# A routed layer's x rows and its results: one transfer over 128 partitions in place of four over 32

## Chip, cores and metric

The program runs on one core of a Trainium2 chip. The metric is the time of one execution on the device, in microseconds (us). The core has five engines with instruction streams of their own: TensorE (PE, with PEld for its weight loads), VectorE (DVE), ScalarE (ACT), GpSimd (POOL) and SyncE (SP). The data between memory and the core's SBUF is moved by 16 DMA engines, which the profile shows as a share of busy time (mean over the 16) and as GB/s.

## What is computed

One layer of a hybrid trunk for 1,024 prompt tokens and 32 sample tokens of 1,024 numbers each. A token mixer (gated linear attention beside differential attention) gives `x1 = x + gate1 * mix`; then a channel mixer takes, for each token, 128 of 16,384 single-neuron experts and adds their weighted sum. Only the second part's frame matters here:

```python
x = x + gt1[:, None, :] * mix
h2 = modulate(x, norm2_gain, sh2, sc2)
ff = peer_ffn(h2.reshape(B * L, D_MODEL), w_pq, sub_keys1, sub_keys2, peer_u, peer_v)
x = x + gt2[:, None, :] * ff.reshape(B, L, D_MODEL)
...
act = jax.nn.gelu(jnp.einsum('td,thkd->thk', xt, peer_u[idx]), approximate=False)
return jnp.einsum('thk,thkd->td', g * act, peer_v[idx])
```

`peer_u` and `peer_v` lie side by side in memory, so that one gathered row of 8 KB has both vectors of an expert.

## The kernel before

The tokens are worked on in nine tiles of up to 128 rows, in five groups (`GROUPS`). The dense part of each group (projections, attention, gates) streams its weights in 1 MB blocks through `NW = 3` buffers `w`, which SyncE refills as TensorE lets go of them (L1742). The routed part is cut into 33 units of 32 tokens (`NU = 33`, `T = 32`). The 128 experts of each of the 32 tokens are spread over 128 partitions: partition `a * 32 + t` has quarter `a` of token `t`'s list (`COPIES = 4`). A unit is 32 gathers (`COLS`), each of 128 rows of 8 KB into one of `RING = 9` slots (`rt_ring`, L1716), issued by GpSimd. Two gathers make a batch, so a unit has `NB = 16` batches.

For each batch VectorE multiplies the gathered `u` halves with the tokens and sums (L1662), ScalarE applies the gelu (L1217), VectorE writes the diagonal matrices (L1673) and TensorE accumulates the `v` halves (L890). With that a pair of slots is free, and GpSimd's wait on `added` ends. The dense work of the next group is laid between the batches by a plan (`sequence`), in a fixed order on each engine, so a late batch also makes the dense work behind it late, and the other way round.

What the change touches is at the edges of a unit. `unit(u)` on SyncE loads what the unit needs: the normed tokens (`rt_h`, L1909), indices and shares (`rt_few_idx`, L1912; `rt_few_prob`, L1915), each in four pieces, and the rows of `x1` (`rt_x`, L1919). The accumulated result of a unit is folded so that partition `a * 32 + t` has columns `a * 256` to `a * 256 + 255` of token `t` (`QC = 256`), and `rt_x` and `rt_y` have the same shape, 128 partitions by 256 numbers. `finish(u)` on VectorE multiplies with the gate and adds `rt_x` (L1687, L1689), in batch 4 of the next unit. `store(u)` on SyncE waits for it and writes `rt_y` to the output (L1926), in batch 6. Before it loads `rt_x` for unit u, SyncE waits until unit u - 2 is finished, since there are two buffers of each. SyncE works off all of this and the weight loads in one queue, in program order.

Of the kernel before, what the change touches and what calls it, by code (L numbers as in the profile page):

```python
# [42 lines left out]
T, COPIES = DEC, P // DEC  # L43
# [3 lines left out]
QC = D // COPIES  # L47
UNITS = [(t * P + j * T, t, j) for t in range(NT) for j in range(COPIES)] + [(SEQ, NT, 0)]
NU = len(UNITS)
# [300 lines left out]
def trunk(nc, d):  # L350
# [15 lines left out]
    with ExitStack() as ctx:  # L366
        def sb(name, shape, dt=F32):
            return ctx.enter_context(nc.sbuf_tensor(name, shape, dt))

        def sem(name, software_dma=False):  # L370
            if software_dma:
                return nc.alloc_semaphore(name)
            used.append(ctx.enter_context(nc.semaphore(name)))
            return used[-1]
# [25 lines left out]
        def area(start, size, *dims):  # L400
            ap = arena[:, start:start + size]
            if len(dims) == 1:
                return ap.rearrange("p (a c) -> p a c", a=dims[0])
            if len(dims) == 2:
                return ap.rearrange("p (a b c) -> p a b c", a=dims[0], b=dims[1])
            return ap
# [18 lines left out]
        x1, h2T = area(0, 2 * D, 2), area(2048, KC * NCOL, KC)  # L425
# [26 lines left out]
        xr = [sb(f"rt_x1{u}", [P, QC]) for u in range(2)]  # L452
        y = [sb(f"rt_y{u}", [P, QC]) for u in range(2)]
# [45 lines left out]
        idx_in, prob_in, tokens_in, rows_in, y_out = ([sem(f"rt_{n}{u}") for u in range(2)]  # L499
                                                      for n in ("idx_in", "prob_in", "tokens_in", "rows_in", "y_out"))  # L500
# [748 lines left out]
        def _(dve):  # L1249
# [415 lines left out]
            def weigh(b):  # L1665
                u, q = b // NB, b % NB
                if q == 0:
                    dve.wait_ge(prob_in[u % 2], 16 * COPIES * (u // 2 + 1))
                dve.wait_ge(gelued, b + 1)
                if b >= 2:  # L1670
                    dve.wait_ge(added, b - 1)
                for i in range(B):
                    dg = nc.vector.tensor_scalar(diag[b % 2][:, i, :], stack, act_dot[:, b % 2, i:i + 1],  # L1673
                                                 few_prob[u % 2][:, q * B + i:q * B + i + 1], ALU.mult, ALU.mult)
                dg.then_inc(weighted, 1)
                if q == 4 and u > 0:
                    finish(u - 1)

            def finish(u):
                i = u % 2  # L1680
                dve.wait_ge(folded, u + 1)
                if u == 0:
                    dve.wait_ge(gate2_in, 16 * 2 * COPIES)
                if u >= 2:
                    dve.wait_ge(y_out[i], 16 * COPIES * (u // 2))
                dve.wait_ge(rows_in[i], 16 * COPIES * (u // 2 + 1))
                nc.vector.tensor_tensor(y[i][:], acc[i][:, 0:QC], gate2[:, 0 if u < NU - 1 else 1, :], ALU.mult).then_inc(gated2, 1)  # L1687
                dve.wait_ge(gated2, u + 1)
                nc.vector.tensor_tensor(y[i][:], y[i][:], xr[i][:], ALU.add).then_inc(y_ready, 1)  # L1689
# [4 lines left out]
            for kind, *args in order("vector"):  # L1694
# [6 lines left out]
                elif kind in stages:  # L1701
                    stages[kind](*args)
            finish(NU - 1)

        @block.gpsimd
# [14 lines left out]
        def _(sp):  # L1720
# [23 lines left out]
            def stored(g):  # L1744

                for i in range(VBUF):
                    sp.wait_ge(v_out[i], 32 * values_stored(g, i))
                for i in range(KBUF):
                    sp.wait_ge(kt_out[i], 16 * (g + 1))
# [150 lines left out]
            def unit(u):  # L1900
                row, t, j = UNITS[u]
                g = [t in tiles for tiles in GROUPS].index(True)
                i = u % 2
                if u >= 2:
                    sp.wait_ge(weighted, (u - 1) * NB)
                for k in range(2):
                    sp.wait_ge(h2_out[k], 16 * sum(s % 2 == k for s in range(GROUPS[g][-1] + 1)))
                sp.wait_ge(x1_out, 16 * (GROUPS[g][-1] + 1))
                sp.dma_start(h2[i][0:T, :], d["h2"][row:row + T]).then_inc(tokens_in[i], 16)  # L1909
                sp.wait_ge(idx_ready, t + 1)  # L1910
                for a in range(COPIES):
                    sp.dma_start(few_idx[i][a * T:(a + 1) * T, :], idx[t % 2][j * T:(j + 1) * T, a * COLS:(a + 1) * COLS]).then_inc(idx_in[i], 16)  # L1912
                sp.wait_ge(prob_ready, t + 1)
                for a in range(COPIES):
                    sp.dma_start(few_prob[i][a * T:(a + 1) * T, :], share[t % 2][j * T:(j + 1) * T, a * COLS:(a + 1) * COLS]).then_inc(prob_in[i], 16)  # L1915
                if u >= 2:
                    sp.wait_ge(y_ready, u - 1)
                for a in range(COPIES):
                    sp.dma_start(xr[i][a * T:(a + 1) * T, :], d["x1"][row:row + T, a * QC:(a + 1) * QC]).then_inc(rows_in[i], 16)  # L1919

            def store(u):
                row = UNITS[u][0]
                sp.wait_ge(y_ready, u + 1)
                dst = d["y_prompt"][0, row:row + T] if u < NU - 1 else d["y_sample"][0]
                for a in range(COPIES):
                    sp.dma_start(dst[:, a * QC:(a + 1) * QC], y[u % 2][a * T:(a + 1) * T, :]).then_inc(y_out[u % 2], 16)  # L1926

            def weigh(b):
                if b % NB == 6 and b // NB > 0:
                    store(b // NB - 1)  # L1930

            stages = {"modrow": modrow, "norm": norm, "dv": dv, "state": store_state, "state2": store_state2, "merge": merge, "mix": mix,
                      "shift": shift, "keys": keys, "gates": gates, "unit": unit, "weigh": weigh}
            for item in order("sync"):
                kind, *args = item
# [4 lines left out]
                for name in finished(item):  # L1940
                    if WPOS[name] + NW < len(WEIGHTS):
                        load_weights(WPOS[name] + NW)
            store(NU - 1)
            sp.wait_ge(y_out[0], 16 * COPIES * ((NU + 1) // 2))
            sp.wait_ge(y_out[1], 16 * COPIES * (NU // 2))
            stored(NG - 1)
            for i in range(3):
                sp.wait_ge(kr_out[i], 16 * max(rows_stored(r) for r in range(NG * 8) if r % 3 == i))
# [78 lines left out]
```

## Time and profile before

| what | value |
|---|---|
| median of 3 runs | 4189.8 us (4176.69 to 4191.25) |
| the profiled execution's own time | 4194.65 us |
| its span | 4192.6 us |
| busy, share of the span | PE 74%, PEld 47%, DVE 65%, ACT 35%, POOL 30% |
| moved | 1499.18 MB, mean 358 GB/s |
| transfers that load `rt_x` | 132 of 32.0 KB |
| transfers that store `rt_y` | 132 of 32.0 KB (128 prompt, 4 sample) |

The busy shares are means over stages with different limits. PE is the engine busiest over the whole span, yet in the last tenth of it PE is busy three tenths of the time. A stretch is bounded by what ends the waits there, so the prediction goes by stretches. A DMA share of 1.00 or a little above means that all 16 engines had a packet in hand all the time (packets overlap a little in the records).

### The profile page before, as it was taken

How to read it: one execution, taken by the hardware profiler on the slowest of the kernel's cores; microseconds unless marked ns; L12 is line 12 of the kernel's file. 1: busy time of each engine (PE TensorE's matmuls, PEld its weight loads, DVE VectorE, ACT ScalarE, POOL GpSimd, SP SyncE). 2: the span in 40 equal slices, each digit the busy share in tenths (PEclk: the TensorE clock that was granted, in tenths of full speed). 3: DMA queues.
4: the chain of work that ended last, by engine and by line, in shares of the span. 5: the costliest groups of instructions: out<-in, count | busy, mean ns of one | idle time of the engine just before them, and what ended most of it. 6: DMA issues, size and time to landing. Idle time of an engine off the chain costs nothing. (4 is left out here: it accounts for less than half of the span.)

```text
span 4192.6 us, 48832 instructions
## 1 busy us (share of the span) xinstructions
PE 3095.6 (74%) x15864; PEld 1988.9 (47%) x15864; DVE 2707.9 (65%) x7617; ACT 1464.8 (35%) x3016; POOL 1241.5 (30%) x1068
## 2 busy tenths in 40 slices
PE   6787798888787769787787789787777686633333
PEld 5677575666555437455554357454343363400000
DVE  2326347337777874578779854697787745887755
ACT  3433356312355660123445630243446611110110
POOL 0000111112233332333333332333333323355453
PEclk8798888899887979888888889898787798855555
DMA  7485767778889999999898999999999999999998
GB/s 268 170 317 180 305 231 272 264 300 336 347 341 369 388 377 394 407 413 402 341 377 351 383 409 392 416 399 397 397 376 382 413 405 414 389 415 415 399 417 335
DMA packets 269364, 1499.18 MB, mean 358 GB/s; under 512 B 44968, under 2 KB 81672, under 8 KB 97464
## 3 DMA queue, kind: packets, MB, share of 16 engines
q0 software_dynamic: 152064, 1107.36, 65.8%
q1 hardware_dynamic: 117048, 388.70, 24.5%
q8 instruction: 128, 2.10, 0.2%
q14 instruction: 124, 1.02, 0.1%
HBM read 1463.49 MB, written 31.36 MB: 357 GB/s over the span
## 5 line engine op out<-in xcount | busy, mean ns | idle before, releaser
L1716 POOL DMA_INDIRECT rt_ring<-in_peer_uv,rt_few_idx x1056 | 1238.1, 1172 | 2922.4 <-PE rt_acc L890 2293.4
L1662 DVE SCALAR_TENSOR_TENSOR rt_ring<-rt_ring,rt_h 128x1024 f32<-128x1024 f32 x1056 | 1266.6, 1220 | 495.3 <-DMA rt_ring<-in_peer_uv,rt_few_idx 488.3
L890 PE MATMUL rt_acc<-rt_ring,rt_diag 128*32 128x512 f32 x4224 | 745.9, 780 | 598.3 <-DVE rt_diag L1673 591.3
L640 PE MATMUL pair<-dense,w 128*128 128x256 f32 (+2 forms) x3056 | 596.6, 354 | 37.3 <-DMA w<-in_weights 35.6
L640 PEld LDWEIGHTS pair<-dense,w 128*128 128x128 f32 x3056 | 516.9, 198 | 149.6 <-issue 62.4
L1217 ACT ACTIVATE rt_act_dot<-rt_dot 128x2 f32<-128x2 f32 x528 | 107.2, 203 | 1299.9 <-DVE rt_ring L1662 1278.0
L629 PE MATMUL pair<-w,dense 128*128 128x256 f32 (+1 forms) x2320 | 548.6, 394 | 5.8 <-DVE dense L1318 2.8
L890 PEld LDWEIGHTS rt_acc<-rt_ring,rt_diag 128*32 128x32 f32 x4224 | 98.9, 121 | 923.9 <-DVE rt_diag L1673 782.3
L629 PEld LDWEIGHTS pair<-w,dense 128*128 128x128 f32 (+1 forms) x2320 | 428.8, 188 | 153.9 <-issue 70.5
L1673 DVE TENSOR_SCALAR rt_diag<-cst,rt_act_dot,rt_few_prob 128x32 f32<-128x32 f32 x1056 | 266.4, 297 | 70.8 <-ACT rt_act_dot L1217 37.8
L640 PE MATMUL bank<-dense,w 128*128 128x256 f32 (+2 forms) x1424 | 281.8, 355 | 19.5 <-DMA w<-in_weights 19.0
L640 PEld LDWEIGHTS bank<-dense,w 128*128 128x128 f32 x1424 | 240.2, 196 | 77.7 <-issue 32.2
L629 PE MATMUL bank<-w,dense 128*128 128x256 f32 (+1 forms) x1136 | 264.6, 389 | 8.5 <-DMA w<-in_weights 4.9
L629 PEld LDWEIGHTS bank<-w,dense 128*128 128x128 f32 (+1 forms) x1136 | 207.3, 185 | 74.2 <-issue 30.8
L1217 ACT ACT_TABLE_LOAD x170 | 218.1, 1283 | 3.0
L799 PE MATMUL pair<-w,dense 64*128 64x512 f32 (+5 forms) x416 | 150.5, 660 | 68.2 <-ACT dense L1156 63.0
L734 PE MATMUL pair<-dense 128*128 128x16 f32 (+1 forms) x528 | 96.3, 329 | 87.1 <-DVE dense L1450 87.1
L734 PEld LDWEIGHTS pair<-dense 128*128 128x128 f32 (+1 forms) x528 | 99.0, 283 | 104.3 <-issue 101.2
L819 PE MATMUL bank<-w,dense 128*128 128x128 f32 (+2 forms) x640 | 123.0, 345 | 29.2 <-DVE dense L1477 28.9
L819 PEld LDWEIGHTS bank<-w,dense 128*128 128x128 f32 (+2 forms) x640 | 102.4, 235 | 63.1 <-issue 61.3
L799 PEld LDWEIGHTS pair<-w,dense 64*128 64x128 f32 (+1 forms) x416 | 65.0, 216 | 133.5 <-issue 124.3
L1156 ACT ACTIVATE dense<-pair,negmax 128x128 f32<-128x128 f32 (+8 forms) x144 | 104.8, 731 | 55.3 <-PE bank L775 40.3
(241 smaller groups left out, 3254.2 us busy)
## 6 DMA issues: line engine op xcount, KB each, us to landing
w<-in_weights SPq DMA_DIRECT2D x284, 1024.0 KB
rt_ring<-in_peer_uv,rt_few_idx POOLq DMA_INDIRECT x1056
dense<-scratch_mod SPq DMA_DIRECT2D x18, 512.0 KB, 11.3
dense<-in_x_prompt SPq DMA_DIRECT2D x16, 512.0 KB
rt_h<-scratch_h SPq DMA_DIRECT2D x33, 128.0 KB
rt_x<-scratch_x SPq DMA_DIRECT2D x132, 32.0 KB
out_k_prompt<-dense SPq DMA_DIRECT2D x32, 128.0 KB
out_v_prompt<-dense SPq DMA_DIRECT2D x32, 128.0 KB, 6.3
```

The lines of the kernel that those rows point to most:

```text
L629: mm = nc.tensor.matmul(bank[b][0:n, 0:CH], src[:, k, c0:c0 + n], wt[:, k * CH:(k + 1) * CH], start=(k == 0), stop=(k == KC - 1))
L640: mm = nc.tensor.matmul(bank[b][:, 0:n], wt[:, k * CH + j * P:k * CH + (j + 1) * P], src[:, k, 0:n], start=(k == 0), stop=(k == KC - 1))
L734: mm = nc.tensor.matmul(bank[b][0:n, i * GBLK:(i + 1) * GBLK], k_blk[:, i, 0:n], e_blk[:, x % 2, i * GBLK:(i + 1) * GBLK], start=True, sto ...
L799: mm = nc.tensor.matmul(pair[m][0:n, o + c:o + c + w], qd[rows, h, c0:c0 + n], keys_of[rows, c:c + w], start=True, stop=True)
L819: mm = nc.tensor.matmul(bank[5][0:n, 0:VD], mixT[0:w, G % 2, (kt - first) * P:(kt - first) * P + n], v[0:w, kt, :], start=(kt == 0), stop= ...
L890: mm = nc.tensor.matmul(acc[u % 2][a * T:(a + 1) * T, :], diag[b % 2][:, i, :], slot[:, D + c * BANK:D + (c + 1) * BANK], start=(q == 0), ...
L1156: nc.scalar.activation(prob[0:n, x % 2, m, 0:nk], pair[m][0:n, o:o + nk], ACT.Exp, bias=negmax[0:n, x % 2, m:m + 1], accum_out=total[0:n, ...
L1217: nc.scalar.activation(act_dot[:, b % 2, :], dot[:, b % 2, :], ACT.Gelu).then_inc(gelued, 1)
L1662: dt = nc.vector.scalar_tensor_tensor(up, up, 1.0, h2[u % 2][:], ALU.mult, ALU.mult, accum_out=dot[:, b % 2, i:i + 1])
L1673: dg = nc.vector.tensor_scalar(diag[b % 2][:, i, :], stack, act_dot[:, b % 2, i:i + 1], few_prob[u % 2][:, q * B + i:q * B + i + 1], ALU.m ...
L1716: nc.gpsimd.indirect_dma_start(ring[n % RING][:], None, d["peer_uv"], bass.IndirectOffsetOnAxis(ap=few_idx[u % 2][:, c:c + 1], axis=0)).th ...
```

## The change

Where four transfers of 32 partitions by 256 numbers each loaded `rt_x`, one now loads all 128 partitions; the memory side is described as a view with the quarter outermost, then the token, then 256 columns. The four stores of `rt_y` are made one in the same way. The counts that are waited for on the two semaphores become a quarter. Bytes and the rows of 1 KB that they are made of stay the same.

```diff
                 if u >= 2:
-                    dve.wait_ge(y_out[i], 16 * COPIES * (u // 2))
-                dve.wait_ge(rows_in[i], 16 * COPIES * (u // 2 + 1))
+                    dve.wait_ge(y_out[i], 16 * (u // 2))
+                dve.wait_ge(rows_in[i], 16 * (u // 2 + 1))
...
                 if u >= 2:
                     sp.wait_ge(y_ready, u - 1)
-                for a in range(COPIES):
-                    sp.dma_start(xr[i][a * T:(a + 1) * T, :], d["x1"][row:row + T, a * QC:(a + 1) * QC]).then_inc(rows_in[i], 16)
+                sp.dma_start(xr[i][:], d["x1"][row:row + T].rearrange("t (a c) -> a t c", a=COPIES)).then_inc(rows_in[i], 16)
...
                 dst = d["y_prompt"][0, row:row + T] if u < NU - 1 else d["y_sample"][0]
-                for a in range(COPIES):
-                    sp.dma_start(dst[:, a * QC:(a + 1) * QC], y[u % 2][a * T:(a + 1) * T, :]).then_inc(y_out[u % 2], 16)
+                sp.dma_start(dst.rearrange("t (a c) -> a t c", a=COPIES), y[u % 2][:]).then_inc(y_out[u % 2], 16)
...
-            sp.wait_ge(y_out[0], 16 * COPIES * ((NU + 1) // 2))
-            sp.wait_ge(y_out[1], 16 * COPIES * (NU // 2))
+            sp.wait_ge(y_out[0], 16 * ((NU + 1) // 2))
+            sp.wait_ge(y_out[1], 16 * (NU // 2))
```

On SyncE, in the middle of the program, this is the end of one unit's loads and the store of the unit before, with what stands between (`w<-in_weights` is a weight block, `dense<-scratch_mod` a row of gains); the shape is that of the side written:

```order
 L1912 DMA rt_few_idx<-rt_idx 32x32 x4
 L1915 DMA rt_few_prob<-rt_prob 32x32 x4
-L1919 DMA rt_x<-scratch_x 32x256 x4
+L1918 DMA rt_x<-scratch_x 128x1x256
 L1742 DMA w<-in_weights 128x2048
 L1873 DMA dense<-scratch_mod 128x1024
-L1926 DMA out_y_prompt<-rt_y 32x256 x4
+L1924 DMA out_y_prompt<-rt_y 4x32x256
 L1880 DMA scratch_h<-dense 128x1024
 L1881 DMA scratch_x<-dense 128x1024
```

Nothing changes place: a weight block still stands behind the load of `rt_x`, and two other stores behind that of `rt_y`, now with one transfer ahead of them where there were four.

At the end of the program SyncE has, before, the last units' loads and stores:

```order
L1926 DMA out_y_prompt<-rt_y 32x256 x4
L1909 DMA rt_h<-scratch_h 32x1024
L1912 DMA rt_few_idx<-rt_idx 32x32 x4
L1915 DMA rt_few_prob<-rt_prob 32x32 x4
L1919 DMA rt_x<-scratch_x 32x256 x4
L1926 DMA out_y_prompt<-rt_y 32x256 x8
L1926 DMA out_y_sample<-rt_y 32x256 x4
```

And with the change:

```order
L1924 DMA out_y_prompt<-rt_y 4x32x256
L1909 DMA rt_h<-scratch_h 32x1024
L1912 DMA rt_few_idx<-rt_idx 32x32 x4
L1915 DMA rt_few_prob<-rt_prob 32x32 x4
L1918 DMA rt_x<-scratch_x 128x1x256
L1924 DMA out_y_prompt<-rt_y 4x32x256 x2
L1924 DMA out_y_sample<-rt_y 4x32x256
```

Again only the counts differ: eight stores of the last two prompt units are two, and the last four are one. The streams of PE, DVE, ACT and POOL are the same before and after.

## Rows read from the trace of the kernel before

**Rows 1.** The page, the DMA engines' busy tenths in 40 slices.

```profile
DMA  7485767778889999999898999999999999999998
```

**Rows 2.** The page, the chain of waits that ended last, shares by engine.

```profile
DMA 19%; PE 14%; DVE 7%; issue 3%; ACT 1%; POOL 1%; SPq 0%; DVEq 0%; ACTq 0%; POOLq 0%
```

**Rows 3.** Windows, instructions on rt_y alone (two a unit); last columns: DMA share, GB/s.

```profile
core 0: us, DVE busy (x), PEclk, DMA share, GB/s
0.00:1500.00 1500.00, 5.05 (x12) 0.86 0.78 294
1500.00:2000.00 500.00, 4.22 (x10) 0.89 0.99 398
2000.00:2400.00 400.00, 2.53 (x6) 0.84 0.92 365
2400.00:2900.00 500.00, 4.22 (x10) 0.90 1.01 404
2900.00:3200.00 300.00, 2.52 (x6) 0.78 0.96 379
3200.00:3700.00 500.00, 3.37 (x8) 0.80 1.01 407
3700.00:4150.00 450.00, 5.06 (x12) 0.50 1.01 412
...
```

**Rows 4.** The chain of waits in the last stretch: start us, us, what.

```profile
4067.76 10.94 DMA rt_ring<-in_peer_uv,rt_few_idx
4082.67 10.94 DMA rt_ring<-in_peer_uv,rt_few_idx
4097.58 11.92 DMA rt_ring<-in_peer_uv,rt_few_idx
```

**Rows 5.** Timeline of SyncE's queue: start us, us, transfers issued.

```profile
3795.82 1.71 SPq L1919 DMA_DIRECT2D rt_x<-scratch_x  x4
3797.57 1.81 SPq L1926 DMA_DIRECT2D out_y_prompt<-rt_y  x4
...
4045.33 1.71 SPq L1919 DMA_DIRECT2D rt_x<-scratch_x  x4
...
4181.91 1.71 SPq L1926 DMA_DIRECT2D out_y_sample<-rt_y  x4
```

**Rows 6.** The page, DMA packets and queues.

```profile
DMA packets 269364, 1499.18 MB, mean 358 GB/s; under 512 B 44968, under 2 KB 81672, under 8 KB 97464
...
q0 software_dynamic: 152064, 1107.36, 65.8%
q1 hardware_dynamic: 117048, 388.70, 24.5%
```

**Rows 7.** DMA issues of SyncE, 48 rows in all, 1171 transfers.

```profile
w<-in_weights SPq DMA_DIRECT2D x284, 1024.0 KB
...
rt_few_idx<-rt_idx SPq DMA_DIRECT2D x132, 4.0 KB
rt_few_prob<-rt_prob SPq DMA_DIRECT2D x132, 4.0 KB
...
scratch_mod<-rt_ring SPq DMA_DIRECT2D x16, 2.0 KB
...
rt_ring<-in_norm_gain SPq DMA_DIRECT2D x8, 2.0 KB
...
w<-scratch_kT SPq DMA_DIRECT2D x8, 16.0 KB
...
rt_ring<-in_b_mod SPq DMA_DIRECT2D x4, 12.0 KB
...
c_raw<-in_c_sample SPq DMA_DIRECT2D x1, 4.0 KB, 1.9
```

**Rows 8.** The chain of waits, two loads of a weight block: start us, us, what.

```profile
2852.95 22.90 DMA w<-in_weights
...
3407.78 23.58 DMA w<-in_weights
```

**Rows 9.** Who waited for whom: us in total, times, longest.

```profile
POOL rt_ring L1716 <- PE rt_acc L890: 2293.4, 485, 25.4
...
DVE rt_ring L1662 <- DMA rt_ring<-in_peer_uv,rt_few_idx: 488.3, 341, 9.4
...
PE pair L640 <- DMA w<-in_weights: 35.6, 5, 17.5
```

## The prediction

> **What bounds the kernel now.** I read the page's row of the DMA engines first [rows 1]: from slice 9 of 40 on it stands at 8 or 9 tenths almost throughout. The chain of waits [rows 2] has DMA as its largest share, 19% against 14% for PE, and most of the DMA part is gathers. Both are averages, so I cut the span into stretches and counted the units in each by the two VectorE instructions on `rt_y` that end a unit [rows 3]. Four stretches are full: 1500 to 2000, 2400 to 2900, 3200 to 3700 and 3700 to 4150, with a DMA share of 0.99 to 1.01. They hold (10 + 10 + 8 + 12) / 2 = 20 of the 33 units. The other 13 lie in stretches at 0.78, 0.92 and 0.96, or end behind 4150.
>
> How a full stretch moves is seen in the chain [rows 4]: a gather is under way for 10.94 us, then a short way over DVE and PE frees its slot, and the next link starts 14.91 us after the last. A gather is 1107.36 MB / 1056 = 1.049 MB [rows 6]; six of them in 14.91 us are 422 GB/s, somewhat above what the full windows show (398 to 412), so a link is six gathers and a gather costs 2.485 us of all engines. The wait rows agree: POOL waits for slots (PE L890, 2293.4 us) and DVE waits for landed gathers (488.3 us), a closed ring with DMA as its slow part [rows 9]. What matters, then, is not how long a transfer of x or y takes, but how much time it takes from the DMA engine that has the most to do.
>
> **Who carries a transfer.** The bytes and the 1 KB rows stay the same: 128 rows for `rt_x` and 128 for `rt_y` in each unit, 16 per DMA engine and unit if all sixteen share them. The question is whether they still do. The page's packets answer it in part [rows 6, 7]. Under 512 B there are 44968. Gathers: 152064 / 1056 = 144 packets each, 128 rows and 16 small ones that can only be the completion on each engine, so 16896 in all. Rows of 128 B: (132 + 132) x 32 for indices and shares and 8 x 128 for the 16 KB weight blocks, 9472; two loads of c with 128 rows of 32 B, 256. That leaves 44968 - 16896 - 9472 - 256 = 18344 completions for SyncE's 1171 transfers. With 16 for each it would be 18736; 392 are missing. 16 + 8 + 4 = 28 transfers have just two rows on their outermost dimension (`scratch_mod`, the gains, the biases), and 28 x 14 = 392. So a transfer with two outermost rows runs on two engines, and those with 32 or 128 on sixteen. The changed transfers have 4 outermost on the memory side and 128 on the SBUF side. No row shows such a mixed one; the two readings are four engines and sixteen. I take four: if either side can only be cut in four, an even deal has four parts.
>
> The Trainium skill (DMA: Bandwidth & Descriptors, section on why a DMA increments its semaphore by 16) states that the number of engines is the largest up to 16 that divides the slowest dimension of both sides, and that they are the lowest-numbered. By that rule it is four, each time the same four; the trace agrees for two rows by the 392 missing completions, and shows nothing for the mixed case.
>
> **The sum.** With four engines each of them carries 64 rows of 1 KB a unit instead of 16: 48 more. The other twelve carry none, but every gather has a part on every engine, so these wait for the four.
> - Price of a 1 KB row, low end: SyncE's queue took 24.5% of 16 x 4192.6 us for 388.70 MB [rows 6], 42.3 us per MB, 0.043 us a row. 48 rows: 2.1 us.
> - High end: in the last stretch three units take 4045.33 - 3795.82 = 249.5 us [rows 5], 83.2 each, where 32 gathers at 2.485 are 79.5. The 3.65 us left hold all that is not gather. Put wholly on the 32 small rows of an engine (16 of x and y, 16 of indices and shares), this is 0.114 us each; 48 rows: 5.5 us.
> - I take 2.5 us, near the low end, since the 3.65 us also hold the token rows, completions and every jitter.
>
> 20 units in full stretches at 2.5 us: +50 us. For the 13 others the windows leave 4 to 22% of the engines' time free, and a lag of 2.5 us in some 100 us can be caught up there; but these windows have full pieces too. I charge a third: 13 x 2.5 / 3 = +11 us. Completions: engines of the four have 2 per unit in place of 8, 20 x 6 at no more than 0.043 us, so between 0 and -5; I take -2. SyncE's issuing: four transfers took 1.71 to 1.81 us [rows 5], a quarter of which is 0.43, so 2.6 us a unit are saved in its queue. What stands behind it there are weight blocks and the stores of the dense part; in full stretches an earlier weight only takes its share of the same engines earlier. I cost it at 0; if that cover is gone it is the third rival below. `rt_x` is wanted by `finish`, a unit and more after its issue, and `rt_y`'s buffer is wanted two units later: a longer transfer is hidden in both. At the end the sample store issues in 0.43 instead of 1.71 us, and four engines move 32 rows each in place of 8, 24 x 0.043 = 1.0 us more: 0.
>
> Sum: 50 + 11 - 2 = +59 us against the profiled execution's own 4194.65 us, 4254. The median lies 4.9 us below that execution, so **4249 us** is predicted for it. The bounds: 20 x 2.1 - 5 = +37, and 20 x 5.5 + 11 = +121, so this case alone ranges from 4222 to 4311.
>
> **Rivals.** Half a per cent (21 us) is about what a measurement here can tell from no change.
> 1. *No change, 4190 us.* The mixed transfer is cut by its 128 partitions and runs on all sixteen; or it runs on four, and the four catch up. For: the load's written side is 128 partitions, and no row shows the mixed case; windows of 0.99 may hold a little idle time. Against: at 1.01 there is nothing to catch up in, and twelve engines' idling is what would show. Chance 0.21.
> 2. *Weights late, about 4340 us.* A weight block often stands right behind x or y on SyncE. On four engines it lines up behind 32 rows in place of 8. If the two queues of an engine take turns row by row, the 24 more cost 24 x (0.043 + 0.327) = 8.9 us, with 0.327 us for a gather's row (65.8% of 16 x 4192.6 us for 135168 rows [rows 6]). A block now takes 22.9 and 23.6 us on the chain [rows 8], three buffers deep, and PE has already waited up to 17.5 us for one [rows 9]. It decides where PE's lead over the weights is under 8.9 us. Ten such units: 10 x 8.9 = +89 on top of the sum. Against: PE's waits for weights are few (5 in that row), and half of the full time has few or no weights. Chance 0.13.
> 3. *Faster, about 4165 us.* SyncE's queue comes 2.6 us a unit earlier to its weight blocks. It needs the first rival's sixteen engines, and PE waiting for a block that was issued late rather than moved late. All 33 units would be 86 us; ten of them, where a block stands right behind and PE waits, are -26. Against: the chain has 0% of SyncE's queue [rows 2]. Chance 0.09. The Trainium skill (same page, Rules for kernel authors) advises to coalesce many small transfers into one large; no row here shows issue time on the path.
>
> **How the numbers follow.** My forecast has 0.57, the rivals 0.21, 0.13 and 0.09. Slower by over 0.5%: 0.57 + 0.13 = 0.70; same 0.21; faster 0.09. A range of 4182 to 4325 leaves out the deeper half of the third rival and most of the second, together under 2 in 10; below it reaches over no change.
>
> **What would show it.** Under four engines SyncE's transfers fall by 198 to 973; the packets of its queue fall from 117048 by 264 x 16 - 66 x 4 = 3960 to 113088 (under sixteen by 3168 to 113880). In the last stretch the distance of two loads of `rt_x` grows from 83.2 to about 85.7 us, and the mean DMA share falls a little below 1.01 though the kernel is slower, since twelve engines idle for what four are behind. Landing times on the chain after an x or y transfer would grow, the 14.91 us links stay. SyncE's issue of x and y falls to about 0.4 us. I am wrong if the packets say sixteen; or if they say four and the unit's pace in the last stretch stays at 83.2 us; or if PE's waits for weights grow by tens of us, which would be the second rival.

## The result, and the profile after

The changed kernel takes 4229.43 us (median of 3 runs, 4226.76 to 4232.46) against 4189.8 us, a ratio of 1.0095 with a 95% interval of 1.0067 to 1.0124. It is slower by 0.95%, 39.6 us. The prediction was 4249 us, slower, with a range of 4182 to 4325. Of the runs below, three single executions (4874 and 10770 us of the layout by unit, 5910 us of the second store by one transfer) are far longer than the others of the same kernel and are left out of the ratios.

The page of the kernel after has the lines that answer to [rows 1] and [rows 6]:

```profile
DMA  7484876788989999999898999999999999999997
...
DMA packets 265404, 1499.16 MB, mean 355 GB/s; under 512 B 41009, under 2 KB 77713, under 8 KB 93505
...
q0 software_dynamic: 152064, 1107.36, 65.9%
q1 hardware_dynamic: 113088, 388.69, 24.3%
```

The row of tenths is almost that of before and tells nothing. The bytes are the same, and SyncE's queue has exactly the 113088 packets that four engines a transfer would give: 3960 fewer than the 117048 of before. Sixteen engines would have left 113880. In the single packet records of that queue, those of 4 B (the completions) are 18344 before, as the prediction counted them, and 14384 after.

Windows of the kernel after, instructions on `rt_y` alone, answering to [rows 3] (the last full stretch taken 30 us longer):

```profile
core 0: us, DVE busy (x), PEclk, DMA share, GB/s
...
1500.00:2000.00 500.00, 4.21 (x10) 0.88 0.99 394
...
2400.00:2900.00 500.00, 4.21 (x10) 0.90 1.01 401
...
3200.00:3700.00 500.00, 3.36 (x8) 0.77 0.99 396
3700.00:4180.00 480.00, 5.06 (x12) 0.51 1.00 400
```

The rate in the four full stretches falls from 398, 404, 407 and 412 GB/s to 394, 401, 396 and 400. In the last it falls by 3% while the mean share falls only from 1.01 to 1.00.

SyncE's queue in that stretch, answering to [rows 5]:

```profile
3814.14 0.58 SPq L1918 DMA_DIRECT2D rt_x<-scratch_x  x1
3814.77 0.62 SPq L1924 DMA_DIRECT2D out_y_prompt<-rt_y  x1
...
4073.12 0.59 SPq L1918 DMA_DIRECT2D rt_x<-scratch_x  x1
...
4213.55 0.54 SPq L1924 DMA_DIRECT2D out_y_sample<-rt_y  x1
```

Three units take 4073.12 - 3814.14 = 259.0 us, 86.3 each, against 83.2. The issue of a transfer of x or y costs 0.54 to 0.62 us in place of 1.71 to 1.81 for four. So SyncE has its saving, and the units are 3.1 us longer.

The packet records of the two traces show what the transfers do in this stretch. Where a store stands right behind a load, the two have 256 rows of 1 KB. Before, these start within 7.5 to 8.3 us. After, it takes 21.3 to 22.2 us, and counted from the first row, the load's four completions come mostly at 7.5 to 12 us and the store's four at 18 to 23 us. The store's rows thus queue behind the load's, on the same four engines. A row itself takes as long as before (median 46 ns). But 64 rows of an engine in 22 us are 0.34 us each, about a row of x or y and a row of a gather (median 312 ns) together, so the two kinds seem to take turns.

The gathers on the chain are late for it, first a row behind a load of before (issued at 4045.33, [rows 5]):

```profile
4051.78 12.00 DMA rt_ring<-in_peer_uv,rt_few_idx
```

Then two links of after, the second with the load issued at 4073.12 ahead of it:

```profile
4064.66 10.95 DMA rt_ring<-in_peer_uv,rt_few_idx
4079.59 13.82 DMA rt_ring<-in_peer_uv,rt_few_idx
```

The short link is still 14.9 us, as in [rows 4], and seven gathers on the chain from 3750 us on take over 13 us, where before it was two.

Where the whole difference arises is read from the instruction that ends a unit. Its rows give the first and the last start in a window; first those of before, for units 0 to 5, 5 to 10, 10 to 13, 13 to 18, 18 to 21, 21 to 25 and 26 to 31 (x is the number of starts, both ends counted; the three figures ahead are durations in ns):

```profile
L1689 DVE TENSOR_TENSOR rt_y<-rt_y,rt_x x6: 424/426/426, 693.3 to 1415.1; 128x256 f32<-128x256 f32 x6
...
L1689 DVE TENSOR_TENSOR rt_y<-rt_y,rt_x x6: 424/426/426, 1415.1 to 1962.3; 128x256 f32<-128x256 f32 x6
...
L1689 DVE TENSOR_TENSOR rt_y<-rt_y,rt_x x4: 424/424/426, 1962.3 to 2312.3; 128x256 f32<-128x256 f32 x4
...
L1689 DVE TENSOR_TENSOR rt_y<-rt_y,rt_x x6: 424/426/426, 2312.3 to 2858.0; 128x256 f32<-128x256 f32 x6
...
L1689 DVE TENSOR_TENSOR rt_y<-rt_y,rt_x x4: 425/426/426, 2858.0 to 3188.4; 128x256 f32<-128x256 f32 x4
...
L1689 DVE TENSOR_TENSOR rt_y<-rt_y,rt_x x5: 424/425/426, 3188.4 to 3627.7; 128x256 f32<-128x256 f32 x5
...
L1689 DVE TENSOR_TENSOR rt_y<-rt_y,rt_x x6: 424/426/426, 3713.8 to 4126.4; 128x256 f32<-128x256 f32 x6
```

The same of the kernel after:

```profile
L1689 DVE TENSOR_TENSOR rt_y<-rt_y,rt_x x6: 425/426/426, 683.9 to 1405.9; 128x256 f32<-128x256 f32 x6
...
L1689 DVE TENSOR_TENSOR rt_y<-rt_y,rt_x x6: 425/426/426, 1405.9 to 1957.6; 128x256 f32<-128x256 f32 x6
...
L1689 DVE TENSOR_TENSOR rt_y<-rt_y,rt_x x4: 425/426/426, 1957.6 to 2306.9; 128x256 f32<-128x256 f32 x4
...
L1689 DVE TENSOR_TENSOR rt_y<-rt_y,rt_x x6: 424/426/426, 2306.9 to 2859.5; 128x256 f32<-128x256 f32 x6
...
L1689 DVE TENSOR_TENSOR rt_y<-rt_y,rt_x x4: 424/426/426, 2859.5 to 3190.5; 128x256 f32<-128x256 f32 x4
...
L1689 DVE TENSOR_TENSOR rt_y<-rt_y,rt_x x5: 424/426/426, 3190.5 to 3642.3; 128x256 f32<-128x256 f32 x5
...
L1689 DVE TENSOR_TENSOR rt_y<-rt_y,rt_x x6: 424/425/426, 3729.2 to 4157.1; 128x256 f32<-128x256 f32 x6
```

In the order of the rows, the pieces last longer after by +0.2, +4.5, -0.7, +6.9, +0.6, +12.5 and +15.3 us; unit 26 adds 0.8 (it ends at 3713.8 and 3729.2) and the last one about 1. In this pair of profiles the full stretches have it all, 40.0 us on 20 units; the other pieces together about 1. A piece by itself is rougher than it looks: with the second store by four transfers, which costs nothing (below), pieces still differ from those of before by up to 3.3 us. The last stretch, where the DMA engines have hardly anything but gathers to carry, has 15.3 / 5 = 3.1 us a unit. Unit 0 ends 9.4 us earlier in the profile of after; that is hardly of the change, since the profiled executions differ there in either direction (with the store alone as one transfer, which first acts behind it, unit 0 ends 12.2 us earlier than before, with the second store by four transfers 2.1 us later). It is why the two spans are only 32.1 us apart.

### The profile page after: what moved, and what is told of

Read it like the earlier page. It is cut to its first block and busy times, and to the rows that moved or that the text cites. A ratio compares the mean times of both kernels' runs of the same rounds, so it can differ in the third digit from the quotient of the medians.

```text
span 4224.7 us, 48634 instructions
## 1 busy us (share of the span) xinstructions
PE 3108.8 (74%) x15864; PEld 1991.9 (47%) x15864; DVE 2706.9 (64%) x7617; ACT 1464.0 (35%) x3016; POOL 1237.4 (29%) x1068
## 3 DMA queue, kind: packets, MB, share of 16 engines
q1 hardware_dynamic: 113088, 388.69, 24.3%
q14 instruction: 124, 1.01, 0.1%
## 5 line engine op out<-in xcount | busy, mean ns | idle before, releaser
L890 PE MATMUL rt_acc<-rt_ring,rt_diag 128*32 128x512 f32 x4224 | 754.9, 789 | 603.4 <-DVE rt_diag L1673 601.0
L1217 ACT ACTIVATE rt_act_dot<-rt_dot 128x2 f32<-128x2 f32 x528 | 106.7, 202 | 1292.5 <-DVE rt_ring L1662 1267.2
```

Source lines behind the costliest of these rows:

```text
L890: mm = nc.tensor.matmul(acc[u % 2][a * T:(a + 1) * T, :], diag[b % 2][:, i, :], slot[:, D + c * BANK:D + (c + 1) * BANK], start=(q == 0), ...
L1217: nc.scalar.activation(act_dot[:, b % 2, :], dot[:, b % 2, :], ACT.Gelu).then_inc(gelued, 1)
```

## The experiments

Theory A: the transfer is dealt to four DMA engines, always the same, and each gather waits for the engine with the most to do; the time follows the rows of that engine, where it has no time to spare. Theory B: weight blocks that stand on SyncE right behind the load are late. Against both: the long transfer itself, SyncE's issuing, or chance.

**The load alone and the store alone.** Each edit is its half of the change; the load's:

```diff
-                for a in range(COPIES):
-                    sp.dma_start(xr[i][a * T:(a + 1) * T, :], d["x1"][row:row + T, a * QC:(a + 1) * QC]).then_inc(rows_in[i], 16)
+                sp.dma_start(xr[i][:], d["x1"][row:row + T].rearrange("t (a c) -> a t c", a=COPIES)).then_inc(rows_in[i], 16)
```

Expected of the load:

> Only the load of rt_x is one transfer; the stores stay four. Theory A (the rows of x and y are dealt to four DMA engines, which then have more to do than the other twelve; the time follows the extra rows of the busiest engine): 24 extra rows a unit in place of 48, so about half of the +40 us of the full change, +20 us (+15 to +25). Packets of SyncE's queue 117048 - 33 x 12 - 33 x 48... that is 132 x 16 completions become 33 x 4, so 115068. Theory B (weight blocks that stand right behind the load of rt_x on SyncE land late, which holds up TensorE; one step of 9.9 us at unit 24 in the changed kernel): the load alone keeps that step, so +25 to +30 us, more than half. Theory C (the four engines don't matter, it is something at the end or the start of the program): 0.

Measured: 1.0072 (1.0054 to 1.0090), 4212.97 us against 4186.17.

Expected of the store:

> Only the store of rt_y is one transfer; the loads stay four. Theory A: also 24 extra rows a unit, +20 us (+15 to +25), the same as with the load alone, and the last stretch's units 1.5 us longer than before. Theory B: the step at unit 24 is gone, so less than half of the change, +10 to +15 us. If a write to memory costs an engine more than a read from it, the store's share is the greater one, +25 or more.

Measured: 1.0034 (1.0019 to 1.0049), 4200.6 us. Both halves cost something, and together (1.06%) they make up the whole. SyncE's queue of the load alone has the packets expected of four engines:

```profile
q1 hardware_dynamic: 115068, 388.70, 24.5%
```

By size this first pair spoke for theory B, +30 and +14 us: both lie just outside the 15 to 25 us that theory A expected of each. So both were run again, beside a kernel that moves the load.

> The run with only the load as one transfer once more, with the same kernel. If its greater price is real, 0.72% again (0.54 to 0.9), +23 to +38 us; if it was chance, about 0.5%, +20 us.

> The run with only the store as one transfer once more, with the same kernel. If its lower price is real, 0.34% again (0.19 to 0.49), +8 to +20 us; if it was chance, about 0.5%, +20 us.

Measured: load 1.0060 (1.0042 to 1.0078), store 1.0042 (1.0024 to 1.0059). The two came closer, and their intervals overlap. Means of both pairs are 0.66% and 0.38%; that the load costs more is likely, not settled.

**The load moved away from the weights.** In the full change first, then with the load alone as one transfer. The old call stays for the first two units only:

```diff
                 if b % NB == 6 and b // NB > 0:
                     store(b // NB - 1)
+                    if b // NB + 1 < NU:
+                        load_rows(b // NB + 1)
```

> The full change, but from the third unit on the load of rt_x for the next unit but one is issued right behind the store of rt_y (batch 6), no longer at the end of the unit's loads, so that no weight block stands between them. The DMA engines' rows are those of the full change. Theory A (busiest engine's rows only): +40 us as in the full change. Theory B (of these, 7 to 10 us are a weight block that is caught behind the load of rt_x at unit 24): the step from unit 23 to 24 falls from 9.9 us to 1 to 3, and the whole to +30 us. A rival: the block behind the pair now stands behind 64 rows on the four engines, and the step only moves elsewhere; then still +40 us with a step of 5 us or more in another place.

Measured: 1.0098 (1.0083 to 1.0113), 4227.54 us against 4188.65, the same as the full change (0.95%) within the intervals, which leave room for some 13 us. The step from unit 23 to 24 (how much later than before unit 24 ends, counted from unit 23) fell from 9.9 to 3.7 us as theory B had it, but others grew (5.7 us at unit 20), and the total did not fall.

> Only the load of rt_x is one transfer, and from the third unit on it is issued right behind the four stores of rt_y, so that no weight block is caught between it and them; the stores stay four. The load at its old place cost 0.72%, the store 0.34%, for the same 24 extra rows a unit. Theory B (the load's greater price is the weight blocks right behind it): now about the store's price, +14 us (+8 to +20). Theory A2 (a load costs more per row on the busiest engine than a store, wherever it stands): still +27 us or more. A rival: the two measurements differ by chance; then the repeats beside this run come closer together, and this one lies between them.

Measured: 1.0047 (1.0029 to 1.0066), between the load (0.66%) and the store (0.38%). That is theory B's side, but the interval reaches to the load's: the two are 8 us apart, and with their intervals it could be none or twice that. Nor did the move act where B expected it. The step from unit 23 to 24 is 5.6 us here, 6.5 and 6.4 us with the load alone at its old place, and 1.2 and 1.5 us with the store alone. What makes the load's step is not shown.

**Two transfers of 64 partitions.** One engine gets more rows, though there are fewer transfers than before:

```diff
-                for a in range(COPIES):
-                    sp.dma_start(xr[i][a * T:(a + 1) * T, :], d["x1"][row:row + T, a * QC:(a + 1) * QC]).then_inc(rows_in[i], 16)
+                for p in range(2):
+                    sp.dma_start(xr[i][2 * p * T:2 * (p + 1) * T, :],
+                                 d["x1"][row:row + T, 2 * p * QC:2 * (p + 1) * QC].rearrange("t (a c) -> a t c", a=2)).then_inc(rows_in[i], 16)
```

and the store likewise.

> Two transfers of 64 partitions each for the load and for the store, with 2 outermost on the memory side. Theory A: each runs on two engines, the same two, so these have 128 rows a unit, 112 more than before. By rows that is 112/48 of the change's +40 us, +93 us (+80 to +150, since less of a longer lag can be caught up), and in the last stretch a unit goes from 83.2 to about 90.5 us. SyncE's queue has 113088 packets again (132 transfers with 2 completions). A rival that holds the transfer as such to be costly (its size or number) expects less than for one transfer, between 0 and +40 us, and 114936 packets if both run on sixteen.

Measured: 1.0272 (1.0251 to 1.0294), 4293.34 us, +114 us by the ratio. Its queue again has the packets of theory A, here of two engines for each of 132 transfers, and the last stretch's five units take 437.9 us:

```profile
q1 hardware_dynamic: 113088, 388.69, 24.1%
```

```profile
L1689 DVE TENSOR_TENSOR rt_y<-rt_y,rt_x x6: 424/426/426, 3782.6 to 4220.5; 128x256 f32<-128x256 f32 x6
```

Who waited for whom, rows of weight blocks, of the same kernel:

```profile
PE pair L640 <- DMA w<-in_weights: 55.1, 9, 15.8
PE bank L640 <- DMA w<-in_weights: 51.6, 4, 21.2
```

A unit there is 87.6 us, 5.1 more than before (82.5): less than the 7.3 us expected. The rest of the 114 us is earlier, in the stretches with dense work, and there PE's waits for weights in these two groups are 106.7 us (before: 35.6 in the first [rows 9] and 19.0 in the second). With two engines, late weights are likely a part of the price; how much of it is not shown. In the packet records the completions of a load and a store come in four pairs here, about 11, 22, 32 and 43 us after the first row: the four transfers go through the same two engines one after the other.

**The same bytes, spread or not.** The store is made a second time, into a scratch tensor, once by four transfers of 32 tokens and once by one:

```diff
+                for a in range(COPIES):
+                    sp.dma_start(d["y2"][row:row + T, a * QC:(a + 1) * QC], y[u % 2][a * T:(a + 1) * T, :]).then_inc(y_out[u % 2], 16)
```

```diff
+                sp.dma_start(d["y2"][row:row + T].rearrange("t (a c) -> a t c", a=COPIES), y[u % 2][:]).then_inc(y_out[u % 2], 16)
```

> The kernel before, with rt_y stored a second time, into a scratch tensor, by four more transfers of 32 tokens on sixteen engines: 8 more rows of 1 KB on each engine a unit, and four more issues on SyncE (57 us in all). Theory A: the time follows the rows of the busiest engine, and the store's price is +14 us for 24 rows, 0.6 us a row: +5 us (0 to +8). A rival in which SyncE's issuing or the number of transfers counts: more than +10 us. One in which the bytes count, whoever carries them: the same as in the run beside it.

> As the run beside it, with the same bytes and the same scratch tensor, but the second store as one transfer with 4 outermost on the memory side: 32 more rows on each of four engines, one more issue. Theory A: 32 rows at the store's 0.6 us a row, +19 us (+14 to +26), four times the run beside it although it issues less. If the bytes count: the same as the run beside it. If the number of transfers counts: less than the run beside it.

Measured: four transfers 1.0003 (0.9988 to 1.0019), one transfer 1.0057 (1.0039 to 1.0074). Four more issues a unit and 4.3 MB more cost nothing that shows; the same bytes in one transfer cost 24 us, as theory A expected. That rules out the bytes and the number of transfers.

**One transfer over sixteen engines.** The scratch copy of `x1` gets the order of the unit's partitions:

```diff
-                    sp.dma_start(d["x1"][t * P:t * P + n], x1[0:n, ti, :]).then_inc(x1_out, 16)
+                    for j in range(n // T):
+                        v = t * COPIES + j
+                        sp.dma_start(d["x1"][v * P:(v + 1) * P].rearrange("(a t) c -> t a c", a=COPIES),
+                                     x1[j * T:(j + 1) * T, ti, :].rearrange("t (a c) -> t a c", a=COPIES)).then_inc(x1_out, 16)
...
+                sp.dma_start(xr[i][:], d["x1"][u * P:(u + 1) * P]).then_inc(rows_in[i], 16)
```

> The scratch copy of x1 is laid out unit by unit, in the order of the partitions, so that the load of rt_x is one transfer with 128 outermost on both sides; the stores of rt_y stay four. It is written in 33 transfers of 32 tokens in place of 9. Theory A: it runs on sixteen engines, none has more to do than before, so no change, 0 (-8 to +8 us). A rival in which one transfer of 128 partitions is itself the cause (a longer transfer ahead of others in the queue): about +20 us. A rival in which SyncE's issuing matters: 99 issues fewer at 0.43 us there, so faster by up to 40 us, and then the change had a gain hidden in it.

Measured: 0.9984 (0.9967 to 1.0000), 4180.15 us. Its queue has 119016 packets: 117048, less 132 x 16 completions, with 33 x 16, 24 x 16 for the additional writes, and 3168 rows more since these are now of 1 KB. That is sixteen engines for the load. A single transfer of 128 partitions is no harm when both sides have 128 outermost. It saves 99 issues and adds 24 for the writes; the net 75 are worth 7 us by the ratio, 14 at the edge of the interval, and perhaps nothing. With whole gathers it is the only version with fewer transfers that loses nothing. The store stayed at four transfers here and was not tried in this way.

**With engines that have time to spare.** Both kernels gather only half of each row, and TensorE takes the `u` half in place of the `v` half, so the second half of the data is left out:

```diff
-                    nc.gpsimd.indirect_dma_start(ring[n % RING][:], None, d["peer_uv"],
+                    nc.gpsimd.indirect_dma_start(ring[n % RING][:, 0:D], None, d["peer_uv"],
```

> The kernel before (four loads, four stores a unit), but each gather brings only the first 4 KB of its rows (the u half), and TensorE takes that half in place of the v half: the second half of the gathered data is left out. The DMA engines then move 554 MB less. Its time is not that of the job; it is the base for the run beside it. It should be 5 to 20% shorter, with the last stretch bound by VectorE and the chain through it, and a DMA share there of 0.6 to 0.8.

> As the run beside it (second half of the gathered data left out), with the load and the store of the full change. Theory A (48 more rows on four engines cost time only where these engines have no time to spare): within 5 us of the run beside it, and the same pace in the last stretch, where the full change costs 3 us a unit. A rival in which the long transfer itself is waited for (finish waits for rt_x, or a later transfer for the queue): the same +40 us, 3 us a unit, as with whole gathers.

Measured: 3838.09 us with four transfers and 3837.37 us with one; the same (ratios to the kernel before 0.9165 both). Windows of the one with four transfers, then of the one with one, instructions on `rt_y`:

```profile
2400.00:2900.00 500.00, 4.19 (x10) 0.90 0.78 275
...
3450.00:3800.00 350.00, 5.05 (x12) 0.51 0.83 278
```

```profile
2400.00:2900.00 500.00, 4.19 (x10) 0.90 0.78 274
...
3450.00:3800.00 350.00, 5.06 (x12) 0.51 0.83 277
```

The five units of the last stretch take 305.4 and 306.9 us, 0.3 us a unit more in place of 3.1. At a DMA share of 0.78 and 0.83, below 1, the 40 us are gone; the intervals of the two ratios leave room for some 14 us. So no wait of `finish` or of a later transfer for the longer one costs time by itself: the price shows only where the four engines have little to spare.

## Why the prediction was right, and what was mis-sized

- *Who carries a transfer*: four engines. Right, by the packet counts (113088 with both transfers merged or in halves, 115068 with one of them merged). The mixed case that no row showed goes by the smaller side here, where 4 and 2 divide 128. The Trainium skill (DMA: Bandwidth & Descriptors, section on why a DMA increments its semaphore by 16) states that the largest number up to 16 is taken that divides the slowest dimension of both sides; the packet counts of all these runs agree. That a load and the store behind it go to the same four is shown by their completions, one group behind the other, in the last stretch; which four they are no record says.
- *The engine with the most to do sets the pace*: right. In the last stretch a unit costs 3.1 us more for 48 rows, 0.064 us a row, between my ends of 0.043 and 0.114 and above my 0.052 (2.5 us). The last stretches of the other runs give 0.04 to 0.08, and with the most rows not the most a row (5.1 us for 112 rows, 0.045).
- *20 units in full stretches at 2.5 us, +50*: the mis-sized term. They gave 40.0 us: 3.1 a unit for the five of the last stretch, 24.7 / 15 = 1.6 for the others, with one step of 9.9 us in it. A share of 0.99 to 1.01 over 400 to 500 us hid gaps: in windows of 25 us of before it falls to 0.84 and 0.94 between 1500 and 2000 us, to 0.91 and 0.94 between 3200 and 3700, and in the last stretch not below 0.97. A lag can be caught up in them; that it is, is argued, and the third full stretch, with gaps too, cost 2.7 us a unit.
- *13 other units at a third, +11*: they gave about 1, though the piece of three units in the window of 0.96 is 5.8 us longer than before with the store alone (2.7 us shorter when that was run again), 8.1 us with the load moved in the full change and 12.5 us with two engines. These two terms are 20 us of the 59; the rest is the 40 us measured.
- *SyncE's saving costed at 0*: right within some us. The layout by unit saves 75 issues for -0.16%, and four more issues a unit cost 0.03%. The saving itself was sized too high: a merged transfer issues in about 0.6 us, not in 0.4, so it is 2.3 us a unit and not 2.6.
- *The lower bound, 4222*, is a slip: +37 us on 4189.8 is 4227.
- *Rival 1 (no change)* is out by the packets and the time, though its second half, catching up, may be what made the price smaller. *Rival 3 (faster)* is out.
- *Rival 2 (weights late)* was priced at +89 us. Its mechanism is there, the small rows and the gathers' rows taking turns, but PE's four largest wait rows for weights grow from 79.6 to 95.1 us in all, not by tens of us. It shows up in one place. The chain of the kernel after has a block issued right behind the load of `rt_x` (the load 3412.13, the block 3412.76), under way for 24.98 us:

```profile
3412.76 24.98 DMA w<-in_weights
```

PE waits 15.3 us for it, in the same unit of before 8.1 us. There the block is issued at 3402.96 and PE's wait for it ends at 3423.00, so its flight is about 5 us longer after. It is also issued 9.8 us later, though unit 23 ends only 4.2 us later. Ahead of the block on the chain of after stands SyncE itself, which issues the unit's tokens, indices, shares and rows from 3406.73 to 3412.72; before, they were issued from 3395.45 on and were not on the chain. So the step is not the flight alone. The windows of the kernel after show the DMA share fall to 0.80, where before it stays at 1.01 or more:

```profile
3399.00:3424.00 25.00, 23.50 (x170) 19.21 (x169) 12.17 (x29) 2.22 (x9) 8.48 (x8) 1.00 1.02 404
3424.00:3449.00 25.00, 11.21 (x64) 8.96 (x64) 5.28 (x14) 0.51 (x2) 1.88 (x2) 0.66 0.80 300
3449.00:3474.00 25.00, 23.70 (x176) 20.26 (x176) 10.28 (x25) 5.14 (x12) 8.41 (x8) 1.00 1.00 410
```

Moving the load in the full change made this step smaller but left the total, so no saving by that move is shown. How much of the full stretches' 24.7 us outside the last goes through late weights, and why the load seems to cost more than the store, stays open.

## What to carry to other kernels

Before merging transfers, look at the outermost size of both sides: here the transfer ran on as many engines as the smaller allowed, and a view that puts 4 outermost took twelve of sixteen away. In a stretch where DMA is full, count the rows of the busiest engine, not the bytes; where it was not (a share of 0.78 to 0.83), the merge cost nothing that showed. If fewer transfers are wanted, change the layout in memory so that 128 is outermost on both sides, and look for gaps in short windows before charging a lag in full; a mean share of 1 over 500 us can hide them.

## What was not expected of the hardware

Issuing one transfer of 128 partitions on SyncE took 0.54 to 0.62 us, where one of the four small ones took about 0.43 us (1.71 for four), so merging four saves 1.1 us and not three quarters of the 1.71. The rows of a load and a store of the last stretch, which start within 8.3 us over sixteen engines, took up to 22.2 us over four, and yet a unit is only 3.1 us longer. The mean DMA share hardly tells of the loss: it fell from 1.01 to 1.00 in the last stretch while the rate fell from 412 to 400 GB/s.
